# A transformer block pair on one core: the first norm by tiles, the router's products between the conditioning's, expert weight pieces behind the first gather

## The chip, the cores and the metric

The kernel runs on one core of a Trainium2 chip. The metric is the device time of one execution in microseconds (us), as the median of several runs. The core has five engines with an instruction stream each: TensorE (PE in the profile; its weight loads are PEld), VectorE (DVE), ScalarE (ACT), GpSimd (POOL) and SyncE (SP). DMAs are issued from SP, ACT and POOL and run on the core's 16 DMA engines.

## What is computed

The reference takes 1024 tokens of width 1024 through a first block and then two layers of a second one, all in float32. What matters here is the beginning of the first block and its mixture of experts:

```
h = rms_norm(x, norm1_g)
proj = h @ w_in                      # q, k, v, recurrent and conformer columns
...                                  # attention, LRU, conformer, w_out, residual
h2 = rms_norm(x, norm2_g)
logits_c, logits_f = h2 @ w_coarse, h2 @ w_fine
grp = argmax(logits_c); top two of the group's 8 fine logits -> expert, gate
order = argsort(expert of each (token, choice)); places in blocks of the experts
y[token] += gate * (silu(h2 @ w_gate[e]) * (h2 @ w_up[e])) @ w_down[e]
```

The second block needs, for each of its two layers, a conditioning `silu(c) @ ada_w + b` of 3072 numbers, for the latents and for the context. It does not depend on the tokens.

## The kernel before, in words

The kernel is one hand-ordered program. Each engine's instructions are written out stage by stage in functions (`norm1_scalar`, `router_tensor` and so on), called in the order of the functions `tensor`, `scalar`, `vector`, `gpsimd` and `sync` at the end of `build`. An engine runs its own list strictly in order; `wait_ge` on a semaphore holds up all that stands behind it on that engine. SP issues nearly all large loads, one queue, in program order.

Float32 products are made of three products of rounded parts (`mm3`, L236): both operands are split in a high part (ACT, a copy that rounds) and a low part (DVE, the difference). For weights that come in pieces of 1 MB the class `Pieces` does this: `fetch` issues the load (L320), `split_scalar` makes the high part (L341, two halves), `split_vector` the low part (L350, two halves), and both first wait for the landing.

**Opening.** `prologue_sync` issues the eight tiles of x (L543, 512 KB each), after the fourth one the constants (L545, 664 KB, of which the identity matrix is the first 64 KB) and the first piece of `w_in` (two DMAs of 512 KB in runs of 512 bytes). `prologue_pool` issues about twenty small loads, most of them of 1 KB or less. The class `Turned` does a norm and turns the rows: `stats_vector` (DVE, L385 to L387 per tile, then one pair L431 and L432 for the four tiles), `stats_scalar` (ACT, the root, L271 and L272), `norm_scalar` and `norm_vector` (even tiles on ACT at L470, odd ones on DVE at L458), `turn_tensor` (PE transposes at L483, block by block of 128 columns, in each block the four tiles), `split_scalar` (L492) and `split_vector` (L516). `norm1_scalar` and `norm1_vector` do tiles 0 to 3 (`half` 0), then the split of the first `w_in` piece, then the split of the turned rows; only then come tiles 4 to 7. TensorE begins with a wait for the constants, transposes, and makes the first product when the first `w_in` piece has both parts.

**Router.** After `w_out` SP loads 12 pieces of the conditioning's weights (two DMAs of 768 KB each, L1482). `norm2_tensor` ends with the router's logits turned back (L1640) and the products of the conditioning's pieces 0 to 8 (`ada_tensor(p, 0, 9)`); each piece is 8 matmuls of 384 columns (16 records of PE at L236). `router_vector` picks the two experts of each token on DVE and sums up (L1737 to L1741). Three small products in `router_tensor` count (`pos`, `tot`), DVE reads the counts at L1743, ranks the experts by size, and builds one-hot matrices of block and slot (L1768 to L1774). `table_tensor` multiplies them (16 matmuls), and `table_vector` makes from it the table `TAB` (L1814) by which POOL gathers the rows of a block (`gather`, L1925), and `TROW` (L1815) for the scatter. Before that `table_vector` splits expert weight piece 0, and behind it pieces 1 and 2. `order_vector` (L1799 to L1803) tells SP which expert has which rank.

**Experts.** The weights come in 192 pieces of 1 MB through a ring of seven places (`RING`), four pieces of gate and up and two of down for a block of one expert. `experts_sync` issues them in order; a piece waits until the one seven before it has been used, and the first seven wait for what lay in their place, as the dictionary `first` says. Pieces 0 to 2 lie where the conditioning's pieces 9 to 11 were. `experts_tensor` turns the gathered rows (L1973), multiplies by gate and up, turns the hidden rows (L2019) and multiplies by down. `turn_vector` makes the low part of the turned rows (L2140).

## Time and profile before

| | |
|---|---|
| median of 3 runs | 2342.57 us (2339.99 to 2343.46) |
| the profiled execution | 2337.69 us, its span 2335.9 us |
| PE busy | 2166.2 us, 93% |
| DVE / ACT / POOL busy | 1352.4 / 1027.7 / 365.1 us |
| granted TensorE clock, mean | 0.975 of full |
| DMA, mean | 149 GB/s |

The span runs from the first instruction to the last; the execution's own time is 1.8 us longer. Engine names in rows are those above; a `q` behind one (SPq, POOLq) is its sequencer, which issues DMAs and waits. `out<-in` are the program's tensors: `mem` is the large on-chip memory, `small` a small one, `r` rounded tiles in it, `psm` the accumulators, `cst` the constants. `[a <-B]` behind a row of the timeline says that the engine was idle for a us before it and what released it. A row with x16 merges 16 like instructions that follow each other, and its duration is that of the whole run.

### The profile page before, as it was taken

What the parts mean: (1) busy time and instruction counts of PE and PEld (TensorE: products, weight loads), DVE (VectorE), ACT (ScalarE), POOL (GpSimd) and SP (SyncE); (2) the same over time, 40 slices, a digit from 0 to 9 for tenths busy, and PEclk for the clock granted to TensorE, in tenths of its full rate; (3) what the DMA queues carried; (4) which work ended last, traced back from release to release, by engine and by line L of the source; (5) the groups of instructions that cost most, each with busy time, mean ns of one, the idle gap of its engine ahead of it and who ended that gap; (6) DMA issues with size and microseconds to landing.
All of it is one profiled execution on the core that took longest, in us unless ns stands there. A gap on an engine that the chain in (4) does not pass through costs nothing.

```text
span 2335.9 us, 26485 instructions
## 1 busy us (share of the span) xinstructions
PE 2166.2 (93%) x10595; PEld 1547.6 (66%) x10595; DVE 1352.4 (58%) x1727; ACT 1027.7 (44%) x1509; POOL 365.1 (16%) x263
## 2 busy tenths in 40 slices
PE   6999999898699998998879999988999999899998
PEld 5877755574585665665568777744555567788886
DVE  5687277453875475474473255566555556543385
ACT  3265366511575465464453234345444523412231
POOL 2000012000210110110100000012555633000014
PEclk9999999998899999999989999999999999999999
DMA  4111030117899999999763011130000031211041
GB/s 128 55 51 40 28 127 28 72 67 300 316 389 412 410 396 394 401 390 406 303 224 84 19 40 29 45 115 1 1 37 1 19 135 73 84 37 54 20 180 64
DMA packets 105743, 348.76 MB, mean 149 GB/s; under 512 B 21944, under 2 KB 54593, under 8 KB 79632
## 3 DMA queue, kind: packets, MB, share of 16 engines
q1 hardware_dynamic: 94896, 321.70, 36.2%
q0 software_dynamic: 9504, 21.08, 2.4%
q10 hardware_dynamic: 1216, 4.24, 0.5%
q8 instruction: 85, 1.39, 0.2%
q14 instruction: 42, 0.34, 0.0%
HBM read 323.21 MB, written 34.26 MB: 153 GB/s over the span
## 4 chain that ended last, share of the span: by engine, by line
PE 76%; DVE 10%; DMA 7%; ACT 5%; issue 2%; SPq 0%; POOL 0%; DVEq 0%; ACTq 0%; POOLq 0%
PE psm L236 72%; DMA mem<-in_exp_w_gate_dram 2%; DVE small L3455 2%; DMA mem<-in_exp_w_up_dram 2%; DVE r L350 1%; PE psm L1109 1%; PE psm L1973 1%; ACT mem L1191 1%; ACT r L341 1%; DMA mem<-in_ada_w_dram 1%; PE psm L483 1%; DMA mem<-in_w_in_dram 1%; PE psm L2019 1%; DMA mem<-in_odd_w_out_dram 1%; DVE mem L3160 0%
## 5 line engine op out<-in xcount | busy, mean ns | idle before, releaser
L236 PE MATMUL psm<-r,r 128*128 128x512 f32 (+3 forms) x6449 | 1545.6, 396 | 76.0 <-DVE r L2140 15.1
L236 PEld LDWEIGHTS psm<-r,r 128*128 128x128 f32 (+2 forms) x6449 | 1191.4, 190 | 414.1 <-issue 92.5
L350 DVE TENSOR_TENSOR r<-mem,r 128x1024 fp32r<-128x1024 f32 (+1 forms) x312 | 360.0, 1198 | 248.5 <-ACT r L341 245.3
L236 PE MATMUL psm<-mem 128*64 128x512 f32 (+11 forms) x2870 | 465.2, 449 | 24.5 <-DMA mem<-in_ada_w_dram 13.5
L341 ACT ACTIVATE r<-mem 128x1024 fp32r<-128x1024 f32 (+1 forms) x312 | 301.5, 1025 | 136.7 <-DMA mem<-in_exp_w_gate_dram 50.8
L236 PEld LDWEIGHTS psm<-mem 128*64 128x64 f32 (+5 forms) x2870 | 205.5, 152 | 222.4 <-issue 162.4
L3669 POOL TENSOR_TENSOR mem<-mem 128x1024 f32<-128x1024 f32 x63 | 152.6, 2421 | 161.8 <-ACT mem L3621 107.1
L3621 ACT ACTIVATE mem<-psm 128x512 f32<-128x512 f32 x160 | 94.4, 595 | 142.1 <-PE psm L236 135.5
L3455 DVE TENSOR_REDUCE small<-psm 128x1 f32<-128x1280 f32 x64 | 95.3, 1488 | 86.5 <-PE psm L236 86.5
L1239 DVE TENSOR_TENSOR_SCAN mem<-mem,small 128x128 f32<-128x128 f32 (+7 forms) x64 | 83.7, 1356 | 24.3 <-POOL mem L1255 20.1
L271 ACT ACTIVATE small<-small 128x1 f32<-128x1 f32 (+2 forms) x31 | 9.1, 294 | 200.6 <-DVE small L387 123.6
L3810 POOL TENSOR_TENSOR mem<-mem 128x1024 f32<-128x1024 f32 (+1 forms) x15 | 35.7, 2381 | 374.8 <-ACT mem L3776 374.8
L236 PE MATMUL psm<-mem,cst 128*128 128x512 f32 (+4 forms) x222 | 79.3, 591 | 1.4 <-ACT mem L2619 1.0
L979 DVE SCALAR_TENSOR_TENSOR mem<-mem,small 128x1024 f32<-128x1024 f32 x60 | 76.9, 1282 | 1.3
L3992 ACT ACTIVATE mem<-psm 128x512 f32<-128x512 f32 x24 | 14.4, 598 | 138.3 <-PE psm L236 138.3
...
L1925 POOL DMA_INDIRECT mem<-h2d,small x26 | 30.8, 1185 | 235.2 <-DVE mem L2157 182.3
L483 PE MATMUL psm<-cst,mem 128*128 128x128 f32 x208 | 35.7, 309 | 30.4 <-ACT mem L470 16.4
L483 PEld LDWEIGHTS psm<-cst,mem 128*128 128x128 f32 x208 | 32.6, 197 | 37.2 <-issue 15.4
L518 DVE TENSOR_TENSOR r<-psm,r 128x256 fp32r<-128x256 f32 (+1 forms) x56 | 26.5, 492 | 49.3 <-ACT r L499 49.2
L1191 ACT ACTIVATE mem<-psm 128x1024 f32<-128x1024 f32 (+3 forms) x48 | 37.2, 811 | 38.0 <-PE psm L236 37.7
L1109 PE MATMUL psm<-cst,mem 128*128 128x128 f32 x288 | 42.7, 284 | 10.4 <-ACT mem L1145 9.6
...
## 6 DMA issues: line engine op xcount, KB each, us to landing
...
```

Source lines behind the costliest of these rows:

```text
L236: return p.e.matmul(o, l, r, start=start, stop=stop, skip_group_check=True)
L341: p.e.activation(h, mem(self.raw(i), [R * n])[:, w * q:w * q + w], ACT.Copy).then_inc(*self.hi_done.up(i, q))
L350: p.e.tensor_tensor(l, mem(self.raw(i), [R * n])[:, w * q:w * q + w], h.bitcast(F32), SUB).then_inc(*self.lo_done.up(i, q))
L483: last = p.e.transpose(ps[:, 128 * j:128 * j + 128], self.tmp[i][:, c::8], cst("ident"))
L979: d = p.e.scalar_tensor_tensor(CA[:, j, :], UPC[:, j, i:i + 1024], tap(j, i), CA[:, j, :], MUL, ADD)
L1109: last = p.e.transpose(ps[:, o:o + 128], KP[s % 3][:, h, 128 * kb:128 * kb + 128], cst("ident"))
L1191: p.e.activation(KP[s % 3][:, :, 512 * c:512 * c + w], PSM[:, 2 * (k % 2):2 * (k % 2) + 2, 0:w], ACT.Sigmoid, scale=-1.0).then_inc(*at_act ...
L1239: p.e.tensor_tensor_scan(keep, keep, zero.broadcast_to([128, n]), 1.0, MUL, ADD).then_inc(*at_dve.up("left", s, h))
L3455: p.e.tensor_reduce(TOP[:, c:c + 1], PSM[:, 5:8, :].rearrange("p a b -> p (a b)")[:, 0:1280], AX, MAX).then_inc(*ml_dve.up("m", u, k))
L3621: p.e.activation(PT[t % 4][:, hd, :], PB.ps("s", t, hd), ACT.Exp, scale=SCALE).then_inc(*ml_act.up("e", t, hd))
L3669: p.e.tensor_tensor(sums, a, PT[t % 4], ADD).then_inc(*ml_pool.up(t))
L3810: p.then(p.e.tensor_tensor(x, x, self.P1[:, s_], MUL), s, "g", i, s_.start)
```

## The change

Opening: the identity is loaded by itself right behind the first tile of x, the other constants after the eighth; the first `w_in` piece follows the fourth tile directly. POOL waits for the fourth tile before its small loads, the first one excepted. Statistics, root and norm of tiles 0 to 3 are done tile by tile on ACT and DVE, and PE transposes tile by tile into all eight banks (`turn_rows_tensor`). PE waits for the identity only; the wait for the other constants stands before `rows_tensor`.

Router: the router's three products come after the conditioning's piece 4 rather than 8, the table's products after piece 9 rather than 11. On DVE the split of expert piece 0 goes behind the table, and `order_vector` moves from behind the first turned rows to right behind the table, ahead of the splits of pieces 0 to 2. SP issues expert piece 3, and with it all behind it, only when the first gather has landed.

```diff
+            def turn_rows_tensor(self, p, half, order=ALL):
+                blocks = self.blocks(half)
+                banks_ = [take(p, self.name, q, c, order=order) for q, c, _ in blocks]
+                for i in self.part(half):
+                    p.wait_ge(*(self.dve if i % 2 else self.act).at("norm", i))
+                    for (q, c, _), ps in zip(blocks, banks_):
+                        j = i - self.g * q
+                        last = p.e.transpose(ps[:, 128 * j:128 * j + 128], self.tmp[i][:, c::8], cst("ident"))
+                        if i == self.part(half)[-1]:
+                            last.then_inc(*self.pe.up(q, c))
...
         def prologue_sync(p):
             for i in range(NT):
                 p.e.dma_start(XIN[i], xs[:, i, :]).then_inc(*x_in[i].up("x"))
-                if i == 3:
-                    p.e.dma_start(CS[:, :], A["k_small"][:, 0:NC - 256]).then_inc(*consts_in.up())
+                if i == 0:
+                    p.e.dma_start(CS[:, 0:128], A["k_small"][:, 0:128]).then_inc(*ident_in.up())
+                elif i == 3:
                     WI.fetch(p, 0)
+            p.e.dma_start(CS[:, 128:NC - 256], A["k_small"][:, 128:NC - 256]).then_inc(*consts_in.up())
...
         def prologue_pool(p):
             p.e.dma_start(g1, A["norm1_g"][0].rearrange("(p c) -> p c", c=8)).then_inc(*g1_in.up())
+            p.wait_ge(*x_in[3].at("x"))
...
-            n1.stats_scalar(p, 0)
-            n1.norm_scalar(p, 0)
+            for i in range(4):
+                n1.stats_scalar(p, (i,))
+                n1.norm_scalar(p, (i,))
             WI.split_scalar(p, 0)
...
-            n1.stats_vector(p, lambda i: [x_in[i].at("x")], 0)
-            n1.norm_vector(p, 0)
+            for i in range(4):
+                n1.stats_vector(p, lambda i: [x_in[i].at("x")], (i,))
+                if i >= 2:
+                    n1.norm_vector(p, (2 * i - 3,))
             WI.split_vector(p, 0)
...
         def project_tensor(p, lru, conf):
-            n1.turn_tensor(p, 0)
+            n1.turn_rows_tensor(p, 0)
             for k, (j, half) in enumerate(CU):
                 if k == 1:
                     n1.turn_tensor(p, 1)
+                    p.wait_ge(*consts_in.at())
                     rows_tensor(p)
...
             last.then_inc(*n2_pe.up("tokens"))
-            ada_tensor(p, 0, 9)
+            ada_tensor(p, 0, 5)
...
         def table_vector(p):
-            WE.split_vector(p, 0)
             p.wait_ge(*rt_pe.at("tab"))
...
             p.e.tensor_copy(TROW, ROW).then_inc(*rt_dve.up("rows"))
-            for i in range(1, 3):
+            order_vector(p)
+            for i in range(3):
                 WE.split_vector(p, i)
...
-            first = {... 3: [ada_pe.at(8)], ...}
+            first = {... 3: [ada_pe.at(8), rows_in[0].at(0)], ...}
...
         def experts_vector(p):
             turn_vector(p, 0)
-            order_vector(p)
             product_vector(p, 0, 0, None)
...
         def tensor(e):
             p = On(e)
-            p.wait_ge(*consts_in.at())
+            p.wait_ge(*ident_in.at())
...
             router_tensor(p)
-            ada_tensor(p, 9, 12)
+            ada_tensor(p, 5, 10)
             table_tensor(p)
+            ada_tensor(p, 10, 12)
             experts_tensor(p)
```

How the lists move, in three places. SP at the start of the program, before and then with the change (`cst` are the constants):

```order
L543 DMA mem<-in_x_dram 128x1024 x4
L545 DMA cst<-in_k_small_dram 128x1328
L320 DMA mem<-in_w_in_dram 128x8x128 x2
L543 DMA mem<-in_x_dram 128x1024 x4
L320 DMA mem<-in_w_in_dram 128x8x128 x2
```

```order
L556 DMA mem<-in_x_dram 128x1024
L558 DMA cst<-in_k_small_dram 128x128
L556 DMA mem<-in_x_dram 128x1024 x3
L320 DMA mem<-in_w_in_dram 128x8x128 x2
L556 DMA mem<-in_x_dram 128x1024 x4
L561 DMA cst<-in_k_small_dram 128x1200
L320 DMA mem<-in_w_in_dram 128x8x128 x2
```

The bulk of the constants now stands behind the first `w_in` piece and behind the last tiles of x.

PE behind the logits, before and then with the change. The rows of 32x384 are the conditioning's (the 4 with `cst` its bias), those of 128x256 and 128x32 the router's, those of 128x42 the table's:

```order
L1640 MATMUL psm<-cst,mem 128x36 x8
L236 MATMUL psm<-mem,cst 32x384 x4
L236 MATMUL psm<-mem 32x384 x32
L236 MATMUL psm<-mem,cst 32x384 x4
L236 MATMUL psm<-mem 32x384 x32
L236 MATMUL psm<-mem,cst 32x384 x4
L236 MATMUL psm<-mem 32x384 x8
L236 MATMUL psm<-r_108,r_111 128x256
L236 MATMUL psm<-r_109,r_111 128x256
L236 MATMUL psm<-r_110,r_111 128x32
L236 MATMUL psm<-mem 32x384 x24
L236 MATMUL psm<-r_112,r_113 128x42 x16
```

```order
L1660 MATMUL psm<-cst,mem 128x36 x8
L236 MATMUL psm<-mem,cst 32x384 x4
L236 MATMUL psm<-mem 32x384 x32
L236 MATMUL psm<-mem,cst 32x384 x4
L236 MATMUL psm<-mem 32x384 x8
L236 MATMUL psm<-r_108,r_111 128x256
L236 MATMUL psm<-r_109,r_111 128x256
L236 MATMUL psm<-r_110,r_111 128x32
L236 MATMUL psm<-mem 32x384 x24
L236 MATMUL psm<-mem,cst 32x384 x4
L236 MATMUL psm<-mem 32x384 x16
L236 MATMUL psm<-r_112,r_113 128x42 x16
```

A piece is 8 matmuls of 32x384 in this list (each is recorded twice in the trace). The router's three products moved ahead of four pieces, the table's sixteen ahead of two.

DVE at the table, before and then with the change (L350 are splits of expert pieces, the first two that of piece 0; the rows from L1810 or L1829 on are the table's):

```order
L350 TENSOR_TENSOR r_90<-mem,r_89 128x1024
L350 TENSOR_TENSOR r_92<-mem,r_91 128x1024
L1810 TENSOR_SCALAR mem<-psm 128x41
L1811 SCALAR_TENSOR_TENSOR mem<-psm,mem 128x41
L1701 TENSOR_SCALAR mem<-mem 128x41
L1702 TENSOR_SCALAR mem<-mem 128x41
L1703 TENSOR_SCALAR mem<-mem 128x41
L1814 CAST small<-mem 128x41
L1815 CAST small<-mem 128x41
```

```order
L1829 TENSOR_SCALAR mem<-psm 128x41
L1830 SCALAR_TENSOR_TENSOR mem<-psm,mem 128x41
L1721 TENSOR_SCALAR mem<-mem 128x41
L1722 TENSOR_SCALAR mem<-mem 128x41
L1723 TENSOR_SCALAR mem<-mem 128x41
L1833 CAST small<-mem 128x41
L1834 CAST small<-mem 128x41
L1819 TENSOR_TENSOR mem<-mem,cst 128x1024
L1821 TENSOR_TENSOR mem<-mem,cst 128x1024
L1822 TENSOR_REDUCE mem<-mem 128x32
L1823 CAST small<-mem 128x30
L350 TENSOR_TENSOR r_90<-mem,r_89 128x1024
```

No split stands ahead of the table any more, and the order of the experts stands ahead of the first split.

## Rows read from the trace of the kernel before

**Rows 1.** The page: shares of the chain that ended last, by engine.

```profile
PE 76%; DVE 10%; DMA 7%; ACT 5%; issue 2%; SPq 0%; POOL 0%; DVEq 0%; ACTq 0%; POOLq 0%
```

**Rows 2.** That chain, 0 to 45 us: start, us, what.

```profile
4.16 13.85 DMA mem<-in_w_in_dram
...
21.48 5.35 DVE r L516 x8
...
32.77 2.36 DVE r L350 x2
```

**Rows 3.** Timeline, 0 to 60 us: start, us, engine, line, operation, idle before.

```profile
2.02 1.06 POOL L552 DMA_DIRECT2D small<-in_q_norm_g_dram  x2
...
4.46 0.69 DVE L385 BATCH_NORM_STATS2 small<-mem 128x6 f32<-128x512 f32 x1 [3.57 <-DMA mem<-in_x_dram]
...
11.11 0.69 DVE L385 BATCH_NORM_STATS2 small<-mem 128x6 f32<-128x512 f32 x1 [1.60 <-DMA mem<-in_x_dram]
...
12.88 0.17 DVE L432 TENSOR_TENSOR small<-small 128x4 f32<-128x4 f32 x1
...
13.71 2.19 ACT L470 ACTIVATE mem<-mem,small 128x1024 f32<-128x1024 f32 x2
...
26.47 2.01 ACT L341 ACTIVATE r<-mem 128x1024 fp32r<-128x1024 f32 x2 [1.81 <-DMA mem<-in_w_in_dram]
...
32.89 0.30 ACT L271 ACTIVATE small<-small 128x4 f32<-128x4 f32 x1 [4.41 <-DVE small L432]
```

**Rows 4.** DMA, 0 to 12 us in 40 slices of 0.3 us; then packets, 12 to 18 us.

```profile
GB/s 0 0 0 0 0 41 109 82 314 314 341 410 369 437 423 423 349 293 396 437 383 219 109 69 55 109 178 109 172 205 221 253 296 341 392 412 318 394 345 352
```

```profile
DMA packets 2458, 1.90 MB, mean 317 GB/s; under 512 B 327, under 2 KB 2250, under 8 KB 2458
```

**Rows 5.** Timeline, 520 to 650 us: conditioning, router and table.

```profile
565.54 1.50 PE L236 MATMUL psm<-mem 128*32 128x384 f32 x16 [1.49 <-DMA mem<-in_ada_w_dram]
...
568.14 0.19 DVE L1741 TENSOR_TENSOR r<-r,r 128x32 fp32r<-128x32 f32 x1
...
583.70 0.65 PE L236 MATMUL psm<-r,r 128*128 128x256 f32 x3
...
584.37 1.50 PE L236 MATMUL psm<-mem 128*32 128x384 f32 x16
584.40 0.19 DVE L1743 COPY mem<-psm 128x32 f32<-128x32 f32 x1 [16.07 <-PE psm L236]
...
598.72 3.57 PE L236 MATMUL psm<-r,r 128*128 128x42 f32 x16 [5.30 <-DVE r L1774]
```

**Rows 6.** Timeline, 600 to 650 us: table, first gather, first products.

```profile
599.33 2.00 ACT L341 ACTIVATE r<-mem 128x1024 fp32r<-128x1024 f32 x2 [0.48 <-DMA mem<-in_exp_w_up_dram]
...
602.15 2.36 DVE L350 TENSOR_TENSOR r<-mem,r 128x1024 fp32r<-128x1024 f32 x2
...
605.65 0.18 DVE L1815 CAST small<-mem 128x41 int32<-128x41 f32 x1
...
606.59 1.33 POOL L1925 DMA_INDIRECT mem<-h2d,small  x1 [52.14 <-DVE small L1815]
...
610.46 1.97 PE L1973 MATMUL psm<-cst,mem 128*128 128x128 f32 x8 [8.17 <-DMA mem<-h2d,small]
...
613.94 10.41 PE L236 MATMUL psm<-r,r 128*128 128x512 f32 x36 [1.51 <-DVE r L2140]
...
618.93 0.33 SPq L320 DMA_DIRECT2D mem<-in_exp_w_down_dram  x1
```

**Rows 7.** DMA, 585 to 620 us in 40 slices of 0.875 us.

```profile
GB/s 416 435 400 421 428 421 426 417 440 421 403 290 337 440 421 412 440 440 421 421 440 403 431 440 393 318 80 127 28 0 42 75 96 32 13 0 0 0 9 7
```

**Rows 8.** All 26 gathers of L1925.

```profile
DMA to landing us min/median/max: 3.8/8.5/9.6
```

**Rows 9.** By stretch: busy us (count) of PE, PEld, DVE, ACT, POOL; clock; DMA share; GB/s.

```profile
570.00:580.00 10.00, 7.08 (x48) 1.49 (x44) 0.00 (x0) 0.32 (x1) 0.00 (x0) 0.52 1.02 418
...
660.00:680.00 20.00, 20.00 (x99) 16.83 (x98) 18.63 (x20) 16.64 (x21) 2.27 (x2) 1.00 1.00 379
...
700.00:720.00 20.00, 20.00 (x95) 9.71 (x92) 6.86 (x7) 8.88 (x12) 2.02 (x2) 1.00 1.00 408
```

**Rows 10.** Timeline of PE, 730 to 760 us: two runs after and without an idle stretch.

```profile
738.33 5.49 PE L236 MATMUL psm<-r,r 128*128 128x512 f32 x12 [2.78 <-DVE r L350]
...
744.81 5.71 PE L236 MATMUL psm<-r,r 128*128 128x512 f32 x24
```

3 lines of the change are left out of this document (2 added, 1 removed).

## The prediction

> **What bounds the kernel now.** The page comes first: the chain that ended last is 76% TensorE [rows 1], so an instruction elsewhere counts only where TensorE waits for it. I then looked for the places where the chain leaves TensorE and the change has a hand in it. There are two.
>
> The first is the opening. The chain starts with the load of the first `w_in` piece, issued at 4.16 us and there 13.85 us later, at 18.01 [rows 2]. ACT and DVE split it, the low parts of the turned rows follow on DVE from 21.48 to 26.83 [rows 2], then statistics, the second piece's split at 32.77 [rows 2], and TensorE is dense from about 40 us. Everything up to there hangs on DVE, and DVE's start hangs on that load. The norm was not the last: its last ACT row ends at 13.71 + 2.19 = 15.90 [rows 3], 2.1 us ahead of the load. Two things delay the load. The constants (664 KB) stand before it. And there is a dip: about 400 GB/s until 6.3 us, then 55 to 220 GB/s for ten slices of 0.3 us [rows 4], in the time when POOL's small loads, issued from 2.02 us on [rows 3], arrive. The fourth tile of x, issued with the first three, is used only at 11.11 [rows 3].
>
> The second place is the router. DVE has its sums at 568.14 + 0.19 = 568.33, needs three products of 0.65 us in all, and gets them only at 584.40, after 16.07 us of idleness [rows 5]. TensorE had four more pieces of the conditioning ahead of them in its list, and those come at the DMA's pace: piece 4 starts at 565.54 and piece 9 at 584.37 [rows 5], 3.77 us apiece. From 584.40 on DVE works without a rest through ranking and one-hot matrices, so the table, the first gather (issued 606.59, turned 610.46) and the first expert product (613.94) are all late by it [rows 6].
>
> **The sum is made against the profiled execution**, 2337.69 us with a span of 2335.9. It lies 4.9 us under the median of the three runs; I take the same difference off the median.
>
> **Opening, -3.4 us.** Data ahead of the first piece's last byte falls from 2.0 + 0.66 + 1 MB to 2.0 + 0.06 + 1 MB. At the 380 or so GB/s of the good slices [rows 4] the 0.6 MB are 1.6 us. The dip costs (400 - 140) / 400 of 3 us, some 2 us. POOL now starts its small loads when the fourth tile is there, so the dip no longer stands before that tile; it moves into the `w_in` piece, whose small runs went at 317 GB/s between 12 and 18 us, beside the small loads of that time [rows 4]. If I start the piece when 2.1 MB are in, at about 7.5 us, and give it the 6 us that it took from 11 to 17 with small loads and some of x between, and the 1 us from last byte to landing, it lands at 14.6, 3.4 us before 18.01. The ends: only the constants count, 1.6; or the piece is faster than that and something else binds. What binds next is DVE's statistics: four tiles from 4.46 [rows 3], each 1.4 us of statistics and 0.4 for the two small operations (the pair ends at 13.05 [rows 3], 0.4 after the statistics), plus a norm of 0.7, then root and norm of the fourth: about 13.9 us, then 8 transposes, some 15.5. That is before the first high part of the rows is due (landing plus 2), so tile by tile is what keeps the norm under the load. It earns nothing by itself, and its six extra small DVE operations are hidden by it. A second limit is the second piece: ACT has its high part at 26.47 + 2.01 = 28.48 [rows 3], by a load whose place in the stream doesn't change, and the root of tiles 4 to 7 stands behind it on ACT, now at 32.89 [rows 3]. So at most 32.89 - 28.48 = 4.4 us can be won. The late constants and columns have their users at 36 us and later. I take 3.4, ends 1.6 and 4.4; from 40 us to 540 TensorE or its partners lead, and the conditioning's loads start when `w_out` is done, so the gain travels with them.
>
> **Router's products, table, gather.** All in the clock of before. TensorE finishes piece 4 at 565.54 + 1.50 = 567.04 and is free when DVE's sums are there; the products end at 568.7, DVE goes on at 568.75 instead of 584.40, 15.65 us earlier, and has its one-hot matrices at 600.4 - 15.65 = 584.75. Pieces 5 to 9 are DMA-paced and end at 584.37 + 1.50 = 585.87, in slow clock perhaps 587.2. Then the table, 3.57 us [rows 5] or less since nothing is waited for in it: done at 588 to 590.9. The table on DVE takes 1.4 us (to 605.83 from the end of the split at 604.5 [rows 6]), POOL another 0.9: the first gather is issued between 590.2 and 593.2, against 606.59, some 15 us earlier.
>
> That gain is not kept. The piece 2 of the ring landed at 599.33 [rows 6], behind the conditioning and pieces 0 and 1, at the DMA's full 420 GB/s [rows 7], and no edit makes it earlier; 1.0 to 1.6 us of gathered rows (one or both first gathers, about 0.4 MB each) now go in between. So it lands at 600.3 to 601. ACT splits it (2.00 us [rows 6]) before it takes up the turned rows, DVE makes its low part (2.36 us [rows 6]) about 1.1 behind, and only then the two low parts of the rows, 1.3 us: landing + 4.85. The other condition is the gather: from landing to product it was 613.94 - 610.46 = 3.48 us [rows 6]. It landed in 3.87 us with the queues nearly idle; under the ring's load the median of all is 8.5 and the longest 9.6 [rows 8]. Issued at 591 and 8.5 later gives 599.5, product at 603. The piece is later: first product at 600.5 + 4.85 = 605.3, a gain of 613.94 - 605.3 = **8.6 us**. Ends: no disturbance of piece 2 gives 604.2, gain 9.8; a piece 2 that lands at 602, or a gather issued at 593.2 that takes 9.6, gives 606.9 or 606.3, gain 7.
>
> **The added wait.** Pieces 3 to 6 landed before 608, when the DMA goes quiet [rows 7]; they will be issued at about 599.5 and land, 2.5 us apiece behind about 4 us of start, at 604, 606.5, 609 and 611.5. SP has nothing but later pieces behind them. The first 24 matmuls use pieces 0 and 1, twelve more piece 2; piece 3 is wanted 10.4 us [rows 6] plus a turn after 605.3, at 616, and is split by 607.5. The others are wanted every 2.9 us from there. Piece 7 is asked for when piece 0 is used up, 5 us after the first product (618.93 against 613.94 [rows 6]), now about 610.3, when piece 6 is just coming in. So I cost the wait at nothing, with a margin of 5 us or more per piece. In the stretch of single experts the DMA moved 379 GB/s where it can do 408 and more [rows 9], so a small backlog is worked off there. `order_vector` (3.9 us on DVE) ran beside the first product and now runs from 591 to 595, before piece 0's high part is complete at 596.4; nobody waits for it.
>
> **Sum.** -3.4 - 8.6 = -12.0: profiled time 2325.7, median 2342.6 - 12.0 = **2330.6 us**. The ends of the terms give -8.6 to -14.2, so 2328.4 to 2334.0.
>
> **A rule weighed.** TensorE was granted 0.52 of its clock, the level of 1.2 GHz, between 570 and 580 us, where it did 16-matmul bursts between loads [rows 9]. After an idle stretch twelve products took 5.49 us, where the 24 after the next turn took 5.71 [rows 10]: 2.6 us lost. The changed kernel idles about 12 us before the first expert product, in place of 8.2 us and 1.5, so I take the first 36 products as they were, 10.41 us. The Trainium skill, page "TensorE: Matmul & The Clock Gate", section on the clock gate, has only these two levels, so that an engine idle for longer restarts no lower; by it the term stays at nothing, and the last rival below has next to no room.
>
> **Rivals.** (a) The DMA stream bounds the experts: its share reads 1.00 throughout [rows 9], so it may be that not TensorE's start but the stream's counts. The stream stood still from about 608 until piece 7 was issued at 618.93, first bytes at about 620; now it has done the same work (pieces to 6, two gathers) at 612 to 613. The gain there would be 7.2 instead of 8.6, the total -10.6: 2332.0. For it: the share; against: 379 GB/s in that stretch is not the DMA's best. Chance 0.15.
> (b) The small loads hurt the `w_in` piece as much as they hurt the tiles: the opening gives 1.6 and the total is -10.2, 2332.4. Chance 0.15.
> (c) The wait does not do what it says: the gather lands before piece 2 anyway, and piece 3 is issued while 2 still runs, so that neither start nor gap changes. Then the experts start at 604.2 to 605.3, total -12 to -13.2: 2329.4 to 2330.6; this is within the forecast's range. The Trainium skill, page "DMA: Bandwidth & Descriptors", Arbitration, says that a DMA engine takes turns between its queues packet by packet; by it the gather would not have had to wait for the weights. No row of before shows a gather beside the first pieces. Chance 0.15.
> (d) Slower. TensorE's clock stays at the low level after the longer idle stretch, and the ring starts with three pieces in hand instead of seven, so that each late piece makes a new pause that keeps it low. At the low level a stretch loses half its length, so to turn -12.0 into +4.7 it would have to last over 33 us longer than before. The restart at 738.33 was over within 12 products [rows 10], which speaks against it. At 40 us it would be +8: 2350. Chance 0.02.
>
> **Chances.** The forecast has 0.53, (a) to (c) 0.45 between them, (d) 0.02. A measurement here tells about 0.2%, 4.7 us, from no change. Of the first four cases only an accumulation of low ends comes near it, so faster 0.93, the same 0.05, slower 0.02. The range takes in the ends of both terms, the rivals (a) and (b) together (-8.8), and 2 us either way for the median: 2326 to 2337.
>
> **What would show it.** In the changed profile: the first ACT row at L341 at about 14.6 instead of 18.03, TensorE dense from about 36.8. The idleness of DVE before the counts about 0.3 instead of 16.07. The gather about 15 us earlier, the first 36 products starting 12 us earlier in all (8.6 of it here), DVE's split of piece 2 as their releaser or just before it. No pause of TensorE in its first 60 us there. From then on everything 12 us earlier to the end. Wrong would be: a pause of TensorE for piece 3 or 4, a gather that takes over 10 us, a first `w_in` split after 16.4, or an end that moved by less than the first expert product did.

## The result, and the profile after

| | kernel before | changed kernel |
|---|---|---|
| median | 2341.28 us (2336.46 to 2343.46, 4 runs) | 2325.14 us (2320.70 to 2325.93, 4 runs) |
| ratio | | 0.9931, 95% interval 0.9916 to 0.9945 |
| the profiled execution | 2337.69 us, span 2335.9 | 2325.93 us, span 2324.1 |
| granted TensorE clock, mean | 0.975 | 0.977 |

The kernel became faster by 0.7%. The forecast of the profiled execution (2325.7) was met to 0.2 us, which is partly luck, as the table of places below shows; that of the median (2330.6, at least 2326) was too high, and the median measured with it lies 0.9 us under the low end. The changed kernel was measured in four more sessions (a session, "call" in the expectations, is a group of kernels that ran side by side on one chip, each with the kernel before beside it). One execution of the kernel before in the session of e5 took 7195.5 us, and the ratios leave it out as slow. All five ratios are 0.9931, 0.9926, 0.9943, 0.9941 and 0.9949; their mean, 0.9938, is 14.5 us of 2341.

**The opening.** The timeline of the changed kernel, 0 to 40 us (start, us, engine, line, operation, idle time before); lines behind L485 have moved down by 12 to 20:

```profile
4.45 0.69 DVE L385 BATCH_NORM_STATS2 small<-mem 128x6 f32<-128x512 f32 x1 [3.55 <-DMA mem<-in_x_dram]
...
7.74 0.69 DVE L385 BATCH_NORM_STATS2 small<-mem 128x6 f32<-128x512 f32 x1 [1.38 <-DMA mem<-in_x_dram]
...
10.65 1.07 POOL L568 DMA_DIRECT2D small<-in_q_norm_g_dram  x2 [8.64 <-DMA mem<-in_x_dram]
...
14.42 0.20 ACT L272 ACTIVATE small<-small 128x1 f32<-128x1 f32 x1
14.65 2.00 ACT L341 ACTIVATE r<-mem 128x1024 fp32r<-128x1024 f32 x2
```

The first `w_in` split starts at 14.65 instead of 18.03, by what was forecast. But there is no idle time before it: it follows the root of the fourth tile on ACT, and the load had landed before. So the opening is now bound by the second tile's landing and DVE's statistics behind it. POOL's small loads begin at 10.65, after 8.64 us of waiting for the fourth tile. The second tile of x was not there until 7.74, after 1.38 us of waiting, and the chain starts with that load:

```profile
1.67 6.05 DMA mem<-in_x_dram
...
18.10 5.35 DVE r L528 x8
...
29.39 2.36 DVE r L350 x2
```

Beside [rows 2], 21.48 has become 18.10 and 32.77 has become 29.39: 3.38 us each.

**The router to the first expert product.** The timeline of 555 to 625 us, which answers to [rows 5, 6]:

```profile
562.55 1.50 PE L236 MATMUL psm<-mem 128*32 128x384 f32 x16 [1.48 <-DMA mem<-in_ada_w_dram]
...
565.68 0.19 DVE L1763 COPY mem<-psm 128x32 f32<-128x32 f32 x1 [0.38 <-PE psm L236]
...
582.82 1.96 PE L236 MATMUL psm<-r,r 128*128 128x42 f32 x16
...
582.95 4.09 SPq L320 DMA_DIRECT2D mem<-in_exp_w_gate_dram  x2
...
585.16 1.50 PE L236 MATMUL psm<-mem 128*32 128x384 f32 x16 [0.38 <-DMA mem<-in_ada_w_dram]
...
587.00 1.33 POOL L1945 DMA_INDIRECT mem<-h2d,small  x1 [35.60 <-DVE small L1834]
...
590.50 3.91 SPq L320 DMA_DIRECT2D mem<-in_exp_w_up_dram  x2
...
591.41 2.00 ACT L341 ACTIVATE r<-mem 128x1024 fp32r<-128x1024 f32 x2 [14.20 <-DMA mem<-in_exp_w_gate_dram]
...
594.11 1.38 PE L1993 MATMUL psm<-cst,mem 128*128 128x128 f32 x8 [3.67 <-DMA mem<-h2d,small]
594.46 0.91 SPq L320 DMA_DIRECT2D mem<-in_exp_w_gate_dram  x2
...
596.42 2.00 ACT L341 ACTIVATE r<-mem 128x1024 fp32r<-128x1024 f32 x2 [0.49 <-DMA mem<-in_exp_w_up_dram]
...
599.86 1.28 DVE L2159 TENSOR_TENSOR r<-psm,r 128x512 fp32r<-128x512 f32 x2
...
601.19 10.31 PE L236 MATMUL psm<-r,r 128*128 128x512 f32 x36 [5.70 <-DVE r L2159]
602.33 2.00 ACT L341 ACTIVATE r<-mem 128x1024 fp32r<-128x1024 f32 x2 [2.56 <-DMA mem<-in_exp_w_up_dram]
```

Piece 4 of the conditioning starts at 562.55 instead of 565.54, the 3 us of the opening. DVE waits 0.38 us for the counts (L1763) instead of 16.07. The table's products take 1.96 us, with no idle time of PE ahead of them. The gather is issued at 587.00, which with the opening's 3.0 us is 590.0 in the clock of before (forecast 590.2 to 593.2), and PE begins to turn the rows at 594.11, 7.1 us later, beside a queue of weights that moves 400 GB/s. Piece 2 of the ring lands at about 596.4; before it was 599.33, so it kept its place behind the opening's 3 us and was not pushed back by the gathered rows. The first product starts at 601.19, piece 2's landing plus 4.77 (forecast 4.85), against 613.94: 12.75 us earlier. It runs its 36 products in 10.31 us without a pause (10.41 before), and piece 3 is split at 602.33. SP's row at 590.50 is the issues of pieces 2 and 3; the second stands at its end, at 594.4, where the gather has come in.

**From there to the end.** Places in seven executions, in us. "Logits" is the ACT row that takes the logits from the accumulators, "last expert" the end of the ring's last eviction.

| execution | logits | first gather turned | first expert product | last expert | span |
|---|---|---|---|---|---|
| before | 546.76 | 610.46 | 613.94 | 1169.39 | 2335.9 |
| before, e13 | 546.79 | 610.35 | 613.82 | 1172.54 | 2340.6 |
| changed | 543.72 | 594.11 | 601.19 | 1153.85 | 2324.1 |
| changed, e5 | 541.88 | 592.35 | 599.42 | 1155.09 | 2328.5 |
| changed, e9 | 542.60 | 594.73 | 601.95 | 1156.55 | 2323.3 |
| changed, e16 | 544.60 | 595.81 | 603.90 | 1162.49 | 2328.9 |
| changed, e18 | 542.23 | 592.51 | 599.60 | 1155.37 | 2328.1 |

In the first pair, 12.75 us at the first product became 15.5 at the last expert and 11.8 at the end. The prediction named an end that moved by less than the first product as a sign of being wrong, and in this pair it is there; in the medians of the five sessions it isn't (14.5 us against 12.75). In the ring the change has one piece of work less, the order of the experts (3.9 us of DVE); in the tail it has no instruction. What went in the tail can be seen on PE, 1360 to 1440 us, first in the changed kernel:

```profile
1368.54 4.50 PE L236 MATMUL psm<-r,r 128*128 128x512 f32 x12
...
1412.97 4.56 PE L236 MATMUL psm<-r,r 128*128 128x512 f32 x12
```

and the same two places before, 15.9 and 14.4 us later:

```profile
1384.45 3.02 PE L236 MATMUL psm<-r,r 128*128 128x512 f32 x12
...
1427.38 3.02 PE L236 MATMUL psm<-r,r 128*128 128x512 f32 x12
```

Twelve products of one shape take 4.5 us rather than 3.0. That is the clock: the granted clock of the changed kernel in the stretches around them (columns as in [rows 9]); before had 1.00 from 1380 to 1480 us:

```profile
1370.00:1380.00 10.00, 10.00 (x78) 7.81 (x76) 7.88 (x12) 5.28 (x8) 0.00 (x0) 0.84 0.01 2
1415.00:1425.00 10.00, 10.00 (x80) 7.79 (x81) 7.72 (x12) 4.74 (x7) 0.00 (x0) 0.87 0.01 2
```

Each such lump costs 1.5 us. They belong to an execution and not to the kernel: e9 and e16 of the same kernel have 3.02 us at both places, e5 and e18 have 4.5 to 4.6 us at both. The tail, from the last expert to the end of the span, goes with them: 1166.4 and 1166.8 us in e16 and e9, 1170.3, 1172.7 and 1173.4 us in the three executions with the two lumps; before and e13, which have neither, took 1166.5 and 1168.1. Over the profiles of all 20 runs the two lumps come together, in seven, whose tails take 1169.3 to 1173.4 us; the other 13 take 1166.4 to 1170.1, so the lumps are the larger part of that scatter but not all of it.

### The profile page after: what moved, and what is told of

Same layout as the page of the kernel before. It is cut to its first block, busy times and chain, and to the rows that moved or that the text cites. A ratio compares the mean times of both kernels' runs of the same rounds, so it can differ in the third digit from the quotient of the medians.

```text
span 2324.1 us, 26500 instructions
## 1 busy us (share of the span) xinstructions
PE 2167.2 (93%) x10595; PEld 1548.2 (67%) x10595; DVE 1353.7 (58%) x1733; ACT 1029.3 (44%) x1515; POOL 365.0 (16%) x263
## 4 chain that ended last, share of the span: by engine, by line
PE 75%; DVE 12%; DMA 7%; ACT 5%; issue 2%; SPq 0%; POOL 0%; DVEq 0%; ACTq 0%; POOLq 0%
PE psm L236 71%; DMA mem<-in_exp_w_gate_dram 2%; DMA mem<-in_exp_w_up_dram 2%; DVE small L3474 2%; DVE r L350 2%; DMA mem<-in_ada_w_dram 1%; DVE mem L999 1%; PE psm L1129 1%; ACT r L341 1%; PE psm L1993 1%; ACT mem L1211 1%; PE psm L483 1%; PE psm L2039 1%; DVE small L385 1%; DVE mem L3179 0%
## 5 line engine op out<-in xcount | busy, mean ns | idle before, releaser
L350 DVE TENSOR_TENSOR r<-mem,r 128x1024 fp32r<-128x1024 f32 (+1 forms) x312 | 360.1, 1198 | 250.3 <-ACT r L341 246.9
L236 PE MATMUL psm<-mem 128*64 128x512 f32 (+11 forms) x2870 | 464.6, 447 | 22.7 <-DMA mem<-in_ada_w_dram 11.8
L3640 ACT ACTIVATE mem<-psm 128x512 f32<-128x512 f32 x160 | 94.4, 596 | 142.0 <-PE psm L236 135.4
L4011 ACT ACTIVATE mem<-psm 128x512 f32<-128x512 f32 x24 | 14.4, 598 | 138.1 <-PE psm L236 138.1
L1129 PE MATMUL psm<-cst,mem 128*128 128x128 f32 x288 | 42.5, 283 | 10.4 <-ACT mem L1165 9.6
L2134 ACT ACTIVATE mem<-psm 128x512 f32<-128x512 f32 x52 | 30.2, 592 | 49.4 <-PE psm L236 49.4
```

What stands on the lines that cost most here:

```text
L236: return p.e.matmul(o, l, r, start=start, stop=stop, skip_group_check=True)
L350: p.e.tensor_tensor(l, mem(self.raw(i), [R * n])[:, w * q:w * q + w], h.bitcast(F32), SUB).then_inc(*self.lo_done.up(i, q))
L1129: last = p.e.transpose(ps[:, o:o + 128], KP[s % 3][:, h, 128 * kb:128 * kb + 128], cst("ident"))
L2134: p.e.activation(YBE[k][:, 512 * o:512 * o + 512], PB.ps("y", n, o), ACT.Copy).then_inc(*moe_act.up("y", n, o))
L3640: p.e.activation(PT[t % 4][:, hd, :], PB.ps("s", t, hd), ACT.Exp, scale=SCALE).then_inc(*ml_act.up("e", t, hd))
```

## The experiments

All times are medians; the ratio is to the kernel before in the same session, with its 95% interval. The five sessions are e1 to e4, e5 to e8, e9 to e12, e13 to e16, and e17 with e18.

| run | kernel | median, us | ratio | first product | last expert |
|---|---|---|---|---|---|
| e1 / e10 | opening alone | 2336.09 / 2337.54 | 0.9988 (0.9976 to 0.9999) / 0.9981 (0.9970 to 0.9992) | 609.60 / 607.93 | 1162.55 / 1161.22 |
| e2 / e11 | router alone | 2331.56 / 2328.81 | 0.9962 (0.9949 to 0.9974) / 0.9947 (0.9928 to 0.9967) | 605.16 / 603.68 | 1160.10 / 1162.01 |
| e3 / e12 | without SP's wait | 2328.70 / 2327.22 | 0.9954 (0.9940 to 0.9968) / 0.9937 (0.9919 to 0.9955) | 599.80 / 599.61 | 1158.32 / 1156.09 |
| e4 | turned rows ahead of piece 2 | 2326.64 | 0.9941 (0.9923 to 0.9958) | 595.82 | 1153.87 |
| e15 / e17 | the same, identity later | 2322.93 / 2326.05 | 0.9930 (0.9914 to 0.9946) / 0.9941 (0.9926 to 0.9956) | 595.96 / 596.85 | 1153.46 / 1150.79 |
| e5, e9, e16, e18 | changed kernel | 2324.51, 2327.60, 2326.40, 2327.97 | 0.9926 (0.9911 to 0.9941), 0.9943 (0.9923 to 0.9963), 0.9941 (0.9925 to 0.9957), 0.9949 (0.9936 to 0.9962) | table above | table above |
| e6 | table after piece 11 | 2327.04 | 0.9949 (0.9934 to 0.9963) | 605.24 | 1158.87 |
| e7 | without POOL's wait | 2327.10 | 0.9941 (0.9928 to 0.9954) | 604.00 | 1160.01 |
| e8 | identity after tile 2 | 2327.78 | 0.9940 (0.9927 to 0.9953) | 599.38 | 1154.28 |
| e13 | before, against itself | 2340.56 | 0.9998 (0.9986 to 1.0009) | 613.82 | 1172.54 |
| e14 | norm not by tiles | 2328.11 | 0.9951 (0.9935 to 0.9966) | 600.69 | 1155.07 |

### The two parts by themselves (e1, e10, e2, e11)

e1 and e10 are the changed kernel with everything from the logits on as before:

```diff
-            ada_tensor(p, 0, 5)
+            ada_tensor(p, 0, 9)
...
+            WE.split_vector(p, 0)
             p.wait_ge(*rt_pe.at("tab"))
...
-            order_vector(p)
-            for i in range(3):
+            for i in range(1, 3):
...
-            first = {... 3: [ada_pe.at(8), rows_in[0].at(0)], ...}
+            first = {... 3: [ada_pe.at(8)], ...}
...
             turn_vector(p, 0)
+            order_vector(p)
...
-            ada_tensor(p, 5, 10)
+            ada_tensor(p, 9, 12)
             table_tensor(p)
-            ada_tensor(p, 10, 12)
```

> The kernel before with the opening of the change alone. Theory A (the two parts add up, each carried unchanged to the end): the first w_in split at 14.65 us as in the changed kernel, conditioning 3.0 us earlier, first expert product at 610.9, the time 3 us under the kernel before. Theory B (part of the 16 us between the medians comes from the opening, which shifts the program against the DMA): 5 to 7 us under it. Theory C (the opening is lost by the DMA-paced stretches behind it): no difference.

> The opening alone again, for the sum: 3 to 4 us under before (theory A and D), first expert product 3 to 4.5 us earlier than in the profile of before.

e2 and e11 are the reverse: the router's part kept, and the whole opening as before, of which these are the main lines:

```diff
-                if i == 0:
-                    p.e.dma_start(CS[:, 0:128], A["k_small"][:, 0:128]).then_inc(*ident_in.up())
-                elif i == 3:
+                if i == 3:
+                    p.e.dma_start(CS[:, :], A["k_small"][:, 0:NC - 256]).then_inc(*consts_in.up())
                     WI.fetch(p, 0)
...
-            p.wait_ge(*x_in[3].at("x"))
...
-            for i in range(4):
-                n1.stats_scalar(p, (i,))
-                n1.norm_scalar(p, (i,))
+            n1.stats_scalar(p, 0)
+            n1.norm_scalar(p, 0)
...
-            n1.turn_rows_tensor(p, 0)
+            n1.turn_tensor(p, 0)
```

> The kernel before with all edits but those of the opening. Theory A: first expert product 9.7 us earlier than before, at 604.2, the time 10 us under the kernel before. Theory B (the expert ring gains by itself, since it now starts with pieces that arrive just in time): the stretch from the first expert product to the last is 2 to 3 us shorter than before as well, the time 12 to 13 us under it.

> All but the opening again, for the sum: 9 to 10 us under before by theories A and D; 12 or more if the ring gains by itself.

The opening alone split its first piece at 14.64 and 14.73 us and had the logits at 543.40 and 541.86, 3.4 and 4.9 ahead of before; in time it gave 2.8 and 4.4 us. The router alone (split at 17.23 and 17.57) had its first product 57.45 and 57.58 us behind the logits where before it was 67.18: 9.7 less. In time it gave 8.9 and 12.4. The means, 3.6 and 10.6, add up to 14.3, and the whole gives 14.5 over its five sessions, so no help or hindrance between the parts is seen. e5 by itself, with 0.9926, would have pointed to more than the sum (its theory B asked for 0.9936 or less); the three later ratios, 0.9941 to 0.9949, don't. The one session that holds both halves and the whole is less tidy: the halves (e10, e11) add up to 16.8 us there, the whole (e9) gave 13.3, 3.5 less, which is more than the 1.5 that e9's first theory allowed, with intervals of 2.6 to 4.7 us either way for each of the three. The two sessions with a part alone differ by 1.6 and 3.5 us, so the split between them is good to about 2 us.

The 67.18 us of before are not fixed either. e1 and e10 have the old router too, and in them the first product came 66.2 and 66.1 us behind the logits. Here are the conditioning's piece 8 in the kernel before and in e1, the piece behind which the old router's products stand:

```profile
580.98 2.79 PE L236 MATMUL psm<-mem 128*32 128x384 f32 x16
```

```profile
577.38 1.50 PE L236 MATMUL psm<-mem 128*32 128x384 f32 x16
```

Before, PE was at the low clock there (granted 0.50 from 578 to 583.7 us), and in e1 piece 8 ran at full speed again, so the counts came some 1.6 us sooner behind the logits, and the first product 1.0 us. Measured from e1 and e10, the router's part is worth 8.6 us at the first product, and measured from the first profile of before and from e13 (67.0) it is 9.5 to 9.7.

### SP's wait for the gather (e3, e12)

```diff
-            first = {... 3: [ada_pe.at(8), rows_in[0].at(0)], ...}
+            first = {... 3: [ada_pe.at(8)], ...}
```

> The changed kernel without the wait of expert piece 3 for the first gather. Theory A (the wait stands behind pieces 0 to 2 in one queue and changes nothing for them): first expert product within 0.5 us of the changed kernel's 601.19, since piece 2's split decides it; the time within 2 us. Theory W (the wait buys the gather): the gather lands more than 3 us later than 594.1, the first product later by 1 us or more. Theory S (the wait is a loss): pieces 3 to 6 land 2 to 3 us earlier than 602.3 to 610 and something after is faster.

> The changed kernel without the wait again, beside the changed kernel. If the wait is worth nothing, it equals the changed kernel within 1.5 us. If the 4 to 6 us between them in two different calls are real, it is 4 us or more slower here as well, although its first expert product was no later (599.80 against 601.19 and 599.42), and the loss must lie in the ring behind it.

Without the wait the gather is no later. The timeline of e3 (POOL issues, PE turns, PE multiplies):

```profile
585.64 1.33 POOL L1945 DMA_INDIRECT mem<-h2d,small  x1 [35.65 <-DVE small L1834]
...
592.73 1.34 PE L1993 MATMUL psm<-cst,mem 128*128 128x128 f32 x8 [3.68 <-DMA mem<-h2d,small]
...
599.80 10.33 PE L236 MATMUL psm<-r,r 128*128 128x512 f32 x36 [5.74 <-DVE r L2159]
```

7.1 us from issue to the turned rows, as with the wait. Even piece 2 is issued after the gather (590.50 behind 587.00 in the changed kernel), so the pieces that the wait holds back would not have stood before the gathered rows anyhow. In time e12 is 0.4 us under the changed kernel of its session. e3's ratio, 0.9954, lies above all five of the changed kernel, but none of them ran in its session. The wait is worth nothing that was measured.

### Where the table stands (e6, beside e5)

```diff
-            ada_tensor(p, 5, 10)
+            ada_tensor(p, 5, 12)
             table_tensor(p)
-            ada_tensor(p, 10, 12)
```

> The changed kernel once more, beside the others of this call. Theory A (the two parts are worth about 12 us; the 16 us between the first medians are 12 us and scatter, four executions each): 11 to 13 us under the kernel before over many executions, ratio 0.9945 to 0.9953. Theory B (they are worth more than their sum at the first expert product): 15 us or more under it, ratio 0.9936 or less.

> The changed kernel with the table's 16 products behind the conditioning's last piece again (after piece 11 instead of 9). Theory A: the table waits for piece 11 (at 588.94 + 1.5 us), so gather issued at about 593 instead of 587, landed at 600 to 601, now behind piece 2's split; first expert product at 604, 2 to 3 us later than in the changed kernel, the time the same 2 to 3 us over it. Rival (the ring's stream sets the end): no difference in the time.

```profile
589.91 1.96 PE L236 MATMUL psm<-r,r 128*128 128x42 f32 x16
590.04 7.98 SPq L320 DMA_DIRECT2D mem<-in_exp_w_up_dram  x2
...
594.09 1.34 POOL L1945 DMA_INDIRECT mem<-h2d,small  x1 [43.06 <-DVE small L1834]
...
596.57 2.01 ACT L341 ACTIVATE r<-mem 128x1024 fp32r<-128x1024 f32 x2 [1.15 <-DMA mem<-in_exp_w_up_dram]
...
597.09 6.89 DVE L350 TENSOR_TENSOR r<-mem,r 128x1024 fp32r<-128x1024 f32 x6
...
597.72 1.97 PE L1993 MATMUL psm<-cst,mem 128*128 128x128 f32 x8 [5.85 <-DMA mem<-h2d,small]
...
605.24 11.24 PE L236 MATMUL psm<-r,r 128*128 128x512 f32 x36 [5.54 <-DVE r L2159]
```

Its DMA, 585 to 605 us in slices of 0.5 us:

```profile
GB/s 393 455 442 422 406 414 393 459 426 410 459 377 410 246 311 393 344 459 213 82 49 33 99 139 41 0 0 197 115 295 295 442 410 377 459 360 467 434 380 437
```

The table's products now wait for piece 11 and are made at 589.91, and the gather is issued 7.1 us later than in the changed kernel. It lands in 3.6 us, about as fast as before with the queues nearly idle. But two things are late by it. DVE, which has the table and then the order of the experts (3.9 us) ahead of its splits, makes the low parts of pieces 0 to 2 only from 597.09 to 603.98, and the turned rows' behind them: the first product comes 61.9 us behind the logits, where it was 57.4 to 59.4 in the five executions of the changed kernel. So most of that delay is the new place of the order of the experts together with the late table; no run parts the two. And here SP's wait shows: piece 3 is issued at 598.0 (the end of the row from 590.04), and the stream falls to nothing at 598. PE did not pause for it in its first 36 products, and what it cost no run tells. The time is 2.5 us more than e5's, with intervals that just overlap. So the table ahead of pieces 10 and 11 pays in the profile, and that SP's wait is harmless because the gather is early is what the rows suggest, without a run of this kernel that leaves the wait out.

### The opening's pieces (e7, e8, e14)

e7 takes POOL's wait away:

```diff
-            p.wait_ge(*x_in[3].at("x"))
```

> The changed kernel without POOL's wait for the fourth tile. If the small loads are what delays the fourth tile, the dip in the DMA's GB/s comes back at 6 to 9 us, the fourth tile's statistics start at 13 us or later instead of 12.16, the first w_in split at 16 instead of 14.65, the time 1.5 us over the changed kernel. If the dip is only the order of the large loads, nothing changes.

DMA of e7, 0 to 12 us in slices of 0.3 us, and its timeline:

```profile
GB/s 0 0 0 0 0 68 123 68 218 328 423 391 332 339 330 341 397 273 150 137 191 219 191 260 232 205 178 205 110 178 233 233 265 265 316 367 358 360 314 314
```

```profile
11.41 0.69 DVE L385 BATCH_NORM_STATS2 small<-mem 128x6 f32<-128x512 f32 x1 [2.28 <-DMA mem<-in_x_dram]
...
13.91 0.69 DVE L385 BATCH_NORM_STATS2 small<-mem 128x6 f32<-128x512 f32 x1
...
17.37 2.00 ACT L341 ACTIVATE r<-mem 128x1024 fp32r<-128x1024 f32 x2 [0.97 <-DMA mem<-in_w_in_dram]
```

The same view of the changed kernel:

```profile
GB/s 0 0 0 0 0 41 205 314 259 300 357 261 195 150 251 247 300 341 274 273 300 300 355 341 382 410 437 416 353 365 331 353 335 318 304 292 294 294 302 323
```

Without the wait, the slices from 5.4 to 9 us stand at 110 to 260 GB/s, the kind of dip that is in [rows 4]; the third tile is waited for until 11.41, and the `w_in` split waits for its load again, until 17.37. With it they are at 273 to 437 from 4.8 us on; a short dip to 150 ahead of that remains. So of the opening's gain of the split (13.2 to 14.9 in the five executions of the changed kernel) 2.4 to 4.2 us are the POOL wait's, though the big constants are already out of the way in e7. The time was 2.6 us above e5, at the edge of what these intervals tell. And 17.37 lies among the four splits of the old opening (17.23 in e2, 17.57 in e11, 17.60 in e13, 18.03): without POOL's wait the rest of the new opening gained nothing that can be told from scatter. What POOL's wait would give by itself, with the constants in their old place, no run shows.

e8 loads the identity behind the second tile:

```diff
-                if i == 0:
+                if i == 1:
                     p.e.dma_start(CS[:, 0:128], A["k_small"][:, 0:128]).then_inc(*ident_in.up())
```

> The changed kernel with the identity behind the second tile of x instead of the first. What sets the first w_in split now is DVE's statistics, idle for 1.38 us at 6.4 us until the second tile lands at 7.7. If the identity's 128 short runs delay that tile, it lands at 6.5 or before, and the split starts 1 us earlier, at 13.6 us; the time 1 us under the changed kernel. If the tile's landing has another cause, nothing changes.

Its split came at 13.42, but that of e5, the changed kernel in the same session, came at 13.22, so this pair shows no gain. All executions together do show that the identity's place matters. DVE's statistics of the second tile in e8:

```profile
6.49 0.68 DVE L385 BATCH_NORM_STATS2 small<-mem 128x6 f32<-128x512 f32 x1
```

There is no idle time before it. The same holds for e15 and e17, which also have the identity behind the second tile, and for the four executions of the old opening (before, e2, e11, e13), which have no identity there: DVE waits for the second tile in none of the seven. Of the 13 executions with the identity behind the first tile it waits in 11, by 0.6 to 1.8 us, and only in e5 and e18 it does not. So the identity between the first two tiles usually delays the second one, though not always; why not always is open. The first split came at 13.4 to 13.5 us in e8, e15 and e17, and at 14.2 on the mean in the five of the changed kernel.

e14 does statistics, root, norm and turning of tiles 0 to 3 as before:

```diff
-            for i in range(4):
-                n1.stats_scalar(p, (i,))
-                n1.norm_scalar(p, (i,))
+            n1.stats_scalar(p, 0)
+            n1.norm_scalar(p, 0)
...
-            n1.turn_rows_tensor(p, 0)
+            n1.turn_tensor(p, 0)
```

> The changed kernel with statistics, root, norm and transposes of tiles 0 to 3 done together again, the new order of loads kept. Theory N (after the loads' reordering the norm is what is last, so tile by tile earns part of the 3.4 us): the first w_in split starts at 15.5 to 16, 1 us or more behind the changed kernel's 13.2 to 14.7, the time 1 us over it. Theory of the prediction (tile by tile earns nothing by itself): the split at 14.6 at the latest and the same time.

```profile
13.05 2.19 ACT L470 ACTIVATE mem<-mem,small 128x1024 f32<-128x1024 f32 x2
15.14 1.99 ACT L341 ACTIVATE r<-mem 128x1024 fp32r<-128x1024 f32 x2
```

Here the norm binds: the split stands behind it on ACT and starts at 15.14, 0.2 to 1.9 us after the changed kernel's. Tile by tile is worth 0.2 to 1.9 us at that place, and in time 1.7 against e16, inside both intervals.

### Is the ring's start all of it (e4, e15, e17), and how far one program scatters (e9, e13, e16, e18)

Since landing of piece 2 plus 4.8 sets the first product, e4 takes the turned rows before that piece on ACT and DVE:

```diff
         def table_vector(p):
-            for i in range(3):
+            for i in range(2):
                 WE.split_vector(p, i)
...
         def experts_scalar(p):
-            for i in range(3):
+            for i in range(2):
                 WE.split_scalar(p, i)
...
             turn_scalar(p, 0)
+            WE.split_scalar(p, 2)
...
             turn_vector(p, 0)
+            WE.split_vector(p, 2)
```

e15 and e17 add to it the identity behind the second tile.

> The changed kernel with the gathered rows turned ahead of the split of expert piece 2 on ACT and DVE. Theory A (what sets the first expert product is piece 2's landing at 596.4 and its split, not the gather, which landed at 594.1): first product at 598.3 to 598.8 instead of 601.19, the time 2.5 us under the changed kernel. Rival (the ring's DMA stream sets the experts' end): the first product is earlier by 2.5 us but the last one is not, and the time is that of the changed kernel.

> The changed kernel with the turned rows ahead of piece 2's split and the identity behind the second tile. Theory R (the DMA stream of the ring sets the end of the experts): first expert product at 596 or before, 4 to 5 us under the changed kernel's, but the last one within 1.5 us of it, and the time within 1.5 us of the changed kernel's. Theory A (what comes at the first product comes at the end): 4 us under it.

> If an earlier first expert product is worth its time at the end, this version (first product about 596, five to eight us ahead of the changed kernel's) is 4 to 6 us faster than the changed kernel in this call. If the ring's stream of weights sets the ring's end, which was 1153 to 1155 us in both so far, it is 0 to 1.5 us faster, and its last expert eviction ends at 1153 to 1156 us again.

```profile
591.25 1.73 PE L1993 MATMUL psm<-cst,mem 128*128 128x128 f32 x8 [3.69 <-DMA mem<-h2d,small]
...
595.82 11.30 PE L236 MATMUL psm<-r,r 128*128 128x512 f32 x36 [2.84 <-DVE r L2161]
```

The first product came 4.57 us after the turn rather than 7.08, at 595.8 to 596.9. In the last expert's end these three have 1152.7 on the mean, the changed kernel's five 1156.7: 4.0 of 5.0 us kept. But 1.8 of the 5.0 stand already at the logits, where the new order of the splits has no part. Counted from the logits the first product comes 3.2 us earlier and the last expert 2.1, and the five of the changed kernel scatter at the last expert by 7.8 us (610.1 to 617.9 behind the logits). In time they are 3.5 us (e15 against e16) and 1.9 us (e17 against e18) ahead, with intervals that overlap in both sessions, and the means of the ratios over all sessions are equal (0.9937 and 0.9938). So whether the ring's stream takes an earlier start back stays open, and a gain of 5 us isn't there. It is the best candidate for a version faster than both, but not one that is shown to be.

> The changed kernel, now on the chip and beside the same executions of before as its two halves. Theory A (adds up): its difference from before equals the sum of the two halves' within 1.5 us. Theory B (the halves help each other): it exceeds the sum by 3 us or more, and the excess shows as shorter stretches behind the pauses of the expert ring in all profiles. Theory D (scatter of executions): its difference changes between calls by 2 us or more, and each profile's excess or lack is made of steps of one size at the ring's pauses.

> The kernel before as a kernel of its own. Theory D (the profiled execution of before was a light one): ratio 1 within its interval, and the profile shows more time than the first one's 2335.9 us, by steps of 1.4 to 1.6 us at places where the twelve products of one group take 4.5 us instead of 3.0, and in the stretches behind the ring's pauses; tail behind the last expert product 1168 to 1171 us instead of 1166.5. Rival (before is always as in its first profile): span within 0.5 us of 2335.9.

> The changed kernel as the anchor of this call: 13 to 17 us under before (ratio 0.993 to 0.9945). Its profile: first expert product 12 to 14.5 us under the first profile of before; the steps of 1.45 us again at some of the named places and not at others.

> The changed kernel once more, as the anchor of this call: by its four earlier ratios 2325 to 2328 us beside 2341 of the kernel before (ratio 0.993 to 0.9945), first expert product at 599 to 604 us, last expert eviction at 1154 to 1162 us.

e13 is the kernel before, run as if it were another. Its ratio is 0.9998, but its profiled execution is 4.7 us longer than the first profile of the same program: 3.3 of it in the ring, 1.5 behind. Of the lumps that its expectation named none stands between 1360 and 1440 us, where every row of twelve products takes 2.99 to 3.06 us; what made it longer is open. The five executions of the changed kernel have spans from 2323.3 to 2328.9. e9 and e16 show one cause of the scatter ahead of the ring. First the conditioning and the table in e9:

```profile
576.59 1.50 PE L236 MATMUL psm<-mem 128*32 128x384 f32 x16 [1.49 <-DMA mem<-in_ada_w_dram]
...
581.77 3.61 PE L236 MATMUL psm<-r,r 128*128 128x42 f32 x16
...
581.89 6.59 SPq L320 DMA_DIRECT2D mem<-in_exp_w_gate_dram  x2
...
585.31 4.36 PE L236 MATMUL psm<-mem 128*32 128x384 f32 x32
...
589.74 5.29 SPq L320 DMA_DIRECT2D mem<-in_exp_w_up_dram  x2
...
594.73 1.97 PE L1993 MATMUL psm<-cst,mem 128*128 128x128 f32 x8 [5.06 <-DMA mem<-h2d,small]
...
597.18 2.00 ACT L341 ACTIVATE r<-mem 128x1024 fp32r<-128x1024 f32 x2 [2.09 <-DMA mem<-in_exp_w_up_dram]
...
601.95 9.73 PEld L236 LDWEIGHTS psm<-r,r 128*128 128x128 f32 x36 [5.65 <-DVE r L2159]
```

and its DMA, 580 to 600 us in slices of 0.5 us:

```profile
GB/s 433 421 406 418 430 442 393 393 442 418 418 422 455 442 406 344 197 98 213 213 262 410 410 377 435 246 320 328 393 295 336 296 141 116 91 117 115 312 426 410
```

In the changed kernel's first profile, in e5 and in e18 TensorE's low-clock stretch fell on two or three of the conditioning's pieces 5 to 8 (2.79 us apiece rather than 1.50; granted clock 0.55 from 570 to 580 us in the first profile), and DMA pace hid it. Here those pieces ran at full clock (1.00), and a low-clock stretch fell on the table: 3.61 us rather than 1.96, with 0.50 granted. Piece 10, behind it on PE, had landed and was used late; ring piece 1 lies in its place, so SP issued it 2.5 us later (6.59 for the two issues against 4.09), and the stream sank to 98 GB/s. Counted from the logits, piece 2 landed 1.9 us later (54.6 against 52.7 us), and the first product came 59.3 us after them, rather than 57.4 or 57.5. e16 is the same to 0.1 us; its first product was 10.0 us earlier than before, where 12 to 14.5 was expected. So, measured from the first profile of before, the router's part is worth 9.5 to 9.8 us in ten of the twelve executions that have it in this order, and 7.8 to 7.9 in two.

## Why the prediction was right and wrong

**Opening, -3.4: size right, mechanism half right.** The split moved by 3.38 us, the logits by 3.04, in the five executions by 2.2 to 4.9, 3.8 on the mean. POOL's small loads were the larger cause, as the dip of [rows 4] suggested, and e7 points to it; the 1.6 us that I gave to the constants no run shows by themselves. But I had the `w_in` load land at 14.6 and set it; it landed before 13.2 in e5, and statistics and root of the fourth tile set it. I had costed that path, with the norm of the fourth tile, at 13.9. It took 13.97 in e5, where DVE waits for no tile after the first, and 15.42 in the first profile, where it waits 1.38 us for the second: the term that I left out is that tile's delay behind the identity. "It earns nothing by itself", of the norm by tiles, holds as far as was measured in time, but rests on too late a load: without it the split stands behind the norm (e14). Rival (b), 1.6 us, is out: the small loads did move into the time of the `w_in` load, without the harm.

**Router, -8.6: right mechanism, undersized by 1.1 us against the profile that I started from.** The counts 15.7 us earlier behind the opening (forecast 15.65), the table without a rest, the landing of piece 2 plus 4.8: all as worked out. The failing term is "1.0 to 1.6 us of gathered rows now go in between": it did not happen, and piece 2 kept its time (52.7 us behind the logits, 52.6 before), which was my no-disturbance end, 9.8 forecast and 9.7 measured. Against e1 and e10 it would be 8.6, so that part of the 9.7 is where the low clock fell in the profile of before. The gather, "8.5 later" by my estimate, took 7.1, and so had no part in it. In the two executions where piece 2 was late, it was so by another road, the clock and the place of piece 10. The Trainium skill, page "DMA: Bandwidth & Descriptors", Arbitration, has a DMA engine take turns between its queues; by that rule, which stood beside rival (c), a gather doesn't queue behind the weights. The landing in 7.1 us beside 400 GB/s doesn't test it: the weights that were issued ahead of the gather had landed by 593.9, 0.2 us before PE took the rows, so a gather that waits for them would look the same.

**The wait: it costs nothing, and brings nothing.** Piece 3 was split at 602.33 in the changed kernel, which is 605.3 in the clock of before (landing forecast at 604), and nobody waited for it. Rival (c) is what happened: the gather lands ahead of piece 2 (594.1 and 596.4), piece 3 is issued at 594.4 while 2 still runs, and e3 and e12 show that without the wait all is the same. Its total, -12 to -13.2, holds the 12.75 measured at the first product, though its median, 2329.4 to 2330.6, is as much too high as mine. I gave it 0.15, and it deserved to be the forecast: piece 2 and the gather both had issue times that could be worked out from the order, and the gather's was the earlier.

**Rival (a), the stream bounds the experts: not what the time shows.** By it the router's part would be 7.2; in time it was 8.9 and 12.4 (intervals of 2.9 and 4.7 us either way, so the first alone would not rule it out), and the last expert's end came 14.3 us earlier on the means (1156.7 against 1171.0), not 10.6. That TensorE's start and not the stream moved it is not shown by this, since the stream moved too (piece 7 was issued 12.9 us earlier). **Rival (d)**: the first 36 products took 10.31 us after the longer pause; no lasting low clock. The mean granted clock over them was 0.81, and 0.80 over the same products before; that doesn't go against the two levels of the Trainium skill, page "TensorE: Matmul & The Clock Gate", section on the clock gate. Where in an execution a low-clock stretch falls, the rows alone tell, and in e9 it cost 1.9 us.

**The step that put the number out of range: "I take the same difference off the median".** It was measured from one profiled execution and moved to the median as if the distance between the two belonged to the kernel. The profiled execution of before lay 4.9 us under the median of its three runs; that of the changed kernel lies 0.8 above its own. So the profiled time fell by 11.8 us (12.0 forecast), and the median by 16.1 in the same session. 2337.69 was a light execution: two of the 20 executions of before in the first session of the experiments were shorter. It has none of the lumps in the tail that e5, e18 or the first profile of the changed kernel have, and e13 shows the same program 4.7 us longer. Of the 4.3 us between 2330.6 and 2326.3, the mean of the five medians, 1.5 are the starting value (2342.57, where the medians of before in those five sessions average 2341.1). The other 2.8 are gain (14.8 between those averages, forecast 12.0): 0.7 of it stands at the first product, whose mean over the five executions is 601.2, 12.7 before 613.9, and 2.1 came behind it. The profiles do not hold those 2.1. From the first product to the last expert the five executions of the changed kernel took 555.5 us on the mean, the two of before 557.1, but e1 and e10, with the old router, 553.0 and 553.3; and the mean span of the five is only 11.7 us under that of the two of before. Where the 2.1 us of the medians come from stays open. The range allowed 2 us for the median either way, and should have allowed for the scatter of a single execution: the 20 profiled executions of all kernels here lie between 8.0 us under (e10) and 5.8 above (e5) the median of their own kernel.
